# Neighbourhood bias as two Toeplitz strips per head and side, doubled tables, and Fourier operands loaded in three portions

## What is computed

```python
rows, kh = 16, 8
rstart = clip(r - kh // 2, 0, rows - kh)          # first of the 8 key rows of query row r
ridx = rstart[:, None] + arange(kh)[None, :]
cstart = clip(col - 8, 0, 64 - 16)                # 16 of the 64 key columns
cmask = (col >= cstart[:, None]) & (col < cstart[:, None] + 16)
dr_i = ridx - r[:, None] + 7
dc_i = clip(col[None, :] - col[:, None] + 15, 0, 30)
bias = rpb[:, dr_i[:, None, :, None], dc_i[None, :, None, :]]
s_loc = einsum(q, k[rows ridx]) * scale + bias    # masked with -1e30 outside cmask
p = softmax(concatenate([s_loc, s_ctx]))          # s_ctx: 512 cached keys, no bias
```

## Time and profile before

| | |
|---|---|
| median of 3 runs | 4331.23 us |
| the profiled execution's own time | 4325.63 us |
| its span | 4324.3 us |
| PE busy | 3974.8 us, 92% of the span |
| DVE, ACT, POOL busy | 2083.2, 902.7, 581.1 us |
| attention, first layer | about 433 us to 1018 us of the span |
| attention, second layer | about 2550 us to 3137 us |

### The profile page before, as it was taken

How to read it: one execution, slowest core, us unless ns; L and a number is a source line. 1 busy time by engine, 2 the same in 40 slices (tenths; PEclk the granted TensorE clock), 3 DMA queues, 4 the chain that set the end, 5 groups by cost and what they waited for, 6 DMA issues and landing times. The chain is left out here.

```text
span 4324.3 us, 48771 instructions
## 1 busy us (share of the span) xinstructions
PE 3974.8 (92%) x19072; PEld 3073.2 (71%) x19072; DVE 2083.2 (48%) x3396; ACT 902.7 (21%) x1700; POOL 581.1 (13%) x484
## 2 busy tenths in 40 slices
PE   5999899788989999999969989988979999999998
PEld 3788556555678888888848965555647888888885
DVE  4121555445265666665542235555444545544454
ACT  2111455343110000000021115543512000000002
POOL 1110111000021111111121110110101111111112
PEclk8999899899999999999979989999989999999999
DMA  6653423563212221111114433255540111110101
GB/s 235 201 161 118 105 52 83 138 170 104 83 52 61 69 69 59 60 57 64 49 30 144 149 102 95 47 130 134 135 153 19 39 40 40 39 40 30 38 31 49
DMA packets 306005, 375.69 MB, mean 87 GB/s; under 512 B 107570, under 2 KB 226228, under 8 KB 305648
## 3 DMA queue, kind: packets, MB, share of 16 engines
q1 hardware_dynamic: 285360, 367.59, 29.1%
q10 hardware_dynamic: 20416, 4.98, 0.5%
HBM read 304.01 MB, written 73.47 MB: 87 GB/s over the span
## 5 line engine op out<-in xcount | busy, mean ns | idle before, releaser
L1922 PE MATMUL bank<-h_hi,w_hi 128*128 128x512 f32 (+1 forms) x2448 | 902.5, 369 | 42.1 <-DVE h_lo L799 38.8
L1923 PE MATMUL bank<-h_lo,w_hi 128*128 128x512 f32 (+1 forms) x2448 | 871.8, 356 | 0.0
L1924 PE MATMUL bank<-h_hi,w_lo 128*128 128x512 f32 (+1 forms) x2448 | 871.2, 356 | 0.0
L2053 PE MATMUL bank<-prob,vv 128*128 128x512 f32 (+3 forms) x1504 | 714.3, 557 | 0.0
L1765 DVE SCALAR_TENSOR_TENSOR xT<-bank,mods,xT 128x512 f32<-128x512 f32 (+1 forms) x816 | 536.6, 660 | 349.2 <-PE bank L1924 331.4
L1922 PE MATMUL bank<-m_hi,w_hi 128*128 128x512 f32 (+1 forms) x1536 | 566.5, 369 | 51.8 <-DVE xT L1765 49.1
L1922 PEld LDWEIGHTS bank<-h_hi,w_hi 128*128 128x128 f32 x2448 | 465.6, 190 | 132.2 <-DVE h_lo L799 40.0
L1924 PE MATMUL bank<-m_hi,w_lo 128*128 128x512 f32 (+1 forms) x1536 | 545.3, 355 | 0.0
L1923 PE MATMUL bank<-m_lo,w_hi 128*128 128x512 f32 (+1 forms) x1536 | 544.6, 355 | 0.0
L1923 PEld LDWEIGHTS bank<-h_lo,w_hi 128*128 128x128 f32 x2448 | 465.4, 190 | 78.6 <-issue 14.5
L1924 PEld LDWEIGHTS bank<-h_hi,w_lo 128*128 128x128 f32 x2448 | 465.0, 190 | 65.9
(11 more groups left out here) (175 smaller groups left out, 4540.8 us busy)
## 6 DMA issues: line engine op xcount, KB each, us to landing
stage<-in_w_mlp SPq DMA_DIRECT2D x64, 1024.0 KB, 5.3
nx_w<-in_w_ada SPq DMA_DIRECT2D x16, 1536.0 KB, 7.1
stage<-in_w_in SPq DMA_DIRECT2D x18, 1024.0 KB, 6.1
ada_h<-in_w_ada SPq DMA_DIRECT2D x16, 1024.0 KB, 8.0
rope_t<-in_k_rope SPq DMA_DIRECT2D x28, 512.0 KB, 4.1
k<-s_kB SPq DMA_DIRECT2D x48, 224.0 KB
k<-s_kA SPq DMA_DIRECT2D x24, 448.0 KB, 10.6
k<-s_kD SPq DMA_DIRECT2D x24, 448.0 KB, 10.7
```

The lines of the kernel that those rows point to most:

```text
L1922: x = pe.matmul(out, a_hi, b_hi, start=first, stop=False)
L1923: pe.matmul(out, a_hi, b_lo, start=False, stop=False)
L1924: return x, pe.matmul(out, a_lo, b_hi, start=False, stop=last)
L2053: pe.matmul(ob[:, q0:q0 + n], vv[h % 2][:, key0 // P], prob[si % NP_RING][:, :n], start=(i == 0 and kind != "D"), stop=(i == len(steps) - ...
```

## The change

**Tables.** Each side of each head is now one table of 24 x 64 = 1536 columns. The first 14 x 64 columns serve query tiles at the edge (128 queries each; tiles 0, 1, 6 and 7), the last 10 x 64 columns the inner tiles (2 to 5). `BIAS_PARTS` lists four loads for each side: two of 64 x 896 and two of 64 x 512. Both sides are held twice, by the parity of the head.

**Work.** A tile at the edge now takes exactly its 512 keys (two pieces of 256 columns in place of two of 320). On the key side one step of each latent half of A shrinks from 512 to 256 queries. A key step that spans edge and inner tiles needs two additions on DVE, one for each strip.

**Order on SP.** All eight bias loads of the next head stand in turns 9 and 10 right behind `load_head`, ahead of the denominators. Ten of the Fourier loads move to the end of turn 8; the other four go in pairs (one of 1024 KB and one of 256 KB) to turns 12 and 13, behind `reciprocals`. The key loads that ended turns 8, 9 and 10 are gone.

```diff
-def na_pattern(t):
-    return {0: 0, 1: 1, 6: 3, 7: 4}.get(t, 2)
+FULL_ROWS, INNER_ROWS = 14, 10
+INNER0 = FULL_ROWS * GRID_W
+TABLE = (FULL_ROWS + INNER_ROWS) * GRID_W
+def at_edge(t):
+    return t in (0, 1, 6, 7)
+def table_col(t, row, key_side):
+    d = 2 * t - row + NA_KH - 1 if key_side else row - 2 * t + NA_KH - 1
+    return (d - 1) * GRID_W if at_edge(t) else INNER0 + (d - 3) * GRID_W
...
-            k0 = key_tile0(tt) * P
-            out += [(t, s, k0 + 320 * s, 320, (na_pattern(tt) * 640 + 320 * s)) for s in range(2)]
+            k0, n = (0 if tt < 2 else LAT // 2, 256) if at_edge(tt) else ((tt - 2) * P, 320)
+            out += [(t, s, k0 + n * s, n, table_col(tt, k0 // GRID_W, False) + n * s) for s in range(2)]
...
-            ts = [t for t in range(4) if key_tile0(4 * c + t) <= kt < key_tile0(4 * c + t) + 5]
+            ts = [t for t in range(4) if (kt // 4 == c if at_edge(4 * c + t) else abs(4 * c + t - kt) <= 2)]
...
+def bias_segments(c, kt, q0, n):
+    ts = range(4 * c + q0 // P, 4 * c + (q0 + n) // P)
+    runs = [[t for t in ts if at_edge(t) == e] for e in (True, False)]
+    return [((r[0] - ts[0]) * P, len(r) * P, table_col(r[0], 2 * kt, True)) for r in runs if r]
...
+BIAS_PARTS = [[(a, 0, 1 - a, FULL_ROWS) for a in range(2)] + [(a, INNER0 + (a + w) * GRID_W, 3 + w, NA_KH) for a in range(2)]
+              for w in range(2)]
...
+            def load_bias(h):
+                for w, tab, sm in ((0, na_q[h % 2], bq_in[h % 2]), (1, na_k[h % 2], bk_in[h % 2])):
+                    for half, c0, r, n in BIAS_PARTS[w]:
+                        sp.dma_start(tab[half * 64:half * 64 + 64, c0:c0 + n * GRID_W],
+                                     s_toe[l, h, w, :, r * GRID_W:(r + n) * GRID_W]).then_inc(sm, 16)
...
                 if v + 1 < NV:
                     load_head(v + 1)
+                if kind == "A" and 1 <= h < 3:
+                    sp.wait_ge(s1_max, l * PIECES + PIECE0[v * NCH])
+                    settle(sp)
+                    sp.wait_ge(s2_add, l * NADD + ADD0[v * NCH])
+                    load_bias(h + 1)
                 if v:
                     denominators_out(v - 1)
...
-                if kind == "A" and 1 <= h < 3:
-                    sp.wait_ge(s1_max, l * PIECES + PIECE0[(v - 1) * NCH + 2])
-                    load_bias(h + 1, 0)
                 if v:
                     reciprocals(v - 1)
-                if kind == "A" and h < 3:
-                    sp.wait_ge(s2_add, l * NADD + ADD0[v * NCH + 1])
-                    load_bias(h + 1, 1)
-                    sp.wait_ge(s2_add, l * NADD + ADD0[v * NCH + 2])
-                    load_bias(h + 1, 2)
+                if kind == "A" and h == 0:
+                    load_fourier()
...
-                    load_fourier()
+                if kind == "D" and h < 2:
+                    load_transform(h)
...
+                    for o, w, col in bias_segments(c, tab, q0, n):
+                        add = dve.tensor_tensor(sb[a % 2][:, o:o + w], bank[:, 2 + si % 3, o:o + w],
+                                                na_k[h % 2][:, col:col + w], ALU.add)
```

More of the change, by code:

```diff
@@ L53 @@
 NADA, NADA1 = 12, 4
[L56 to L62, removed]
 def constants():
@@ L531, in trunk @@
     off = W0
[L532 to L536, removed]
+    na_q, na_k = [], []
+    for s in range(2):
+        for lst, nm in ((na_q, "na_q"), (na_k, "na_k")):
+            a, off = at(f"{nm}{s}", [P, TABLE], F32, off)
+            lst.append(a)
+    off = W0 + 36864
     o_b, off = at("o_b", [P, 2, TOK], F32, off)
@@ L552, in trunk @@
     f_col, _ = at("f_col", [P, 2], F32, o + 32)
-    na_q1.append(put("na_q1b", [P, 2 * 640]))
+    cur["c"] += 2 * 640 * 4
     g_neg, _ = at("g_neg", [P, 2, 256], F32, cur["c"])
@@ L612, in trunk @@
     rest_in = [sem(f"rest_in{i}") for i in range(2)]
-    b_in = [sem(f"b_in{i}") for i in range(4)]
+    bq_in = [sem(f"bq_in{i}") for i in range(2)]
+    bk_in = [sem(f"bk_in{i}") for i in range(2)]
     b_init = sem("b_init")
@@ L966, in load_fourier, with load_transform @@
                 sp.dma_start(dft_col, I["k_dft_col"]).then_inc(f_in, 16)
[L967 to L969 removed]
+            def load_transform(x):
+                sp.dma_start(dft_t[:, x], I["k_dft_lat"][x].rearrange("(t p) n -> p t n", p=P)).then_inc(f_in, 16)
+                sp.dma_start(dft_x[:, x], I["k_dft_ctx"][x].rearrange("(t p) n -> p t n", p=P)).then_inc(f_in, 16)
             def load_head(v):
@@ L1185, in _ @@
             barrier(pool, l * PHASES + 1)
-            for tab in (na_q0, na_q1[0], na_q1[1], na_k[0], na_k[1]):
+            for tab in na_q + na_k:
                 pool.memset(tab, NEG).then_inc(b_init, 1)
@@ L1622, in _, with table_ready @@
             dve.wait_ge(lam_d, l * 5 + 5)
-            def table_ready(kind, h, which):
-                if kind == "A" and which == 0:
-                    n = 16 * len(BIAS_PARTS[0])
-                    dve.wait_ge(b_in[0 if h % 2 == 0 else 3], l * 2 * n + (h // 2 + 1) * n)
-                elif kind == "A":
-                    n = 16 * len(BIAS_PARTS[which])
-                    dve.wait_ge(b_in[which], l * 4 * n + (h + 1) * n)
+            def table_ready(sm, h):
+                n = 16 * len(BIAS_PARTS[0])
+                dve.wait_ge(sm[h % 2], l * 2 * n + (h // 2 + 1) * n)
             def piece(j, p):
@@ L1646, in piece @@
                 else:
-                    table_ready(kind, h, 0)
-                    table = q_table(h, tab, n) if kind == "A" else swa_q[:, tab:tab + n]
+                    if kind == "A":
+                        table_ready(bq_in, h)
+                    table = (na_q[h % 2] if kind == "A" else swa_q)[:, tab:tab + n]
                     if gi >= 2:
```

50 lines of the change are left out of this document (11 added, 39 removed).

## The result

| | before | after |
|---|---|---|
| median, timed side by side, 4 runs each | 4330.01 us (4328.18 to 4331.52) | 4279.46 us (4274.02 to 4281.96) |
| ratio | | 0.9879, 95% interval 0.9864 to 0.9894 |
| span of the profiled execution | 4324.3 us | 4280.6 us |

What follows compares the result with a forecast made beforehand. PE was taken as the bound, busy 92% of the span, with gaps from DVE waiting on late transfers. Terms 1 to 5 less term 6 gave 60.6 us, for a median of 4271 us, range 4250 to 4300.

Steps and rivals of the forecast that it cites:

- Term 1: Turns 9 and 10: `den_c` at T + 22.1 (T: previous head's scores done), not T + 28.8; 26.8 us.
- Term 2: Turn 11: head's loads wait only for six stores, `den_c` at T + 19.9, not T + 25.2; 10.6 us.
- Term 3: Turn 13: fewer Fourier loads ahead, `den_c` at T + 21.1, not T + 26.2; 10.2 us in both layers.
- The residual stalls of PE: PE's remaining stalls in turns 9 and 10, forecast at 3 to 5 us.
- term 5: PE in attention: narrower steps and pieces save 12 us of work, 7.5 us of it on the path.
- term 4: PE after stalls: shorter stalls give back half of 16 us lost to the low clock, 8 us.
- Term 6: DVE in A heads: 64 split additions cost 9.8 us, of which 2.5 us shows as loss.
- (a): Turns 9 and 10: bias loads cost `den_c` only 3 us and the clock does not fall; 4250 us; chance 0.15.
- (b): SP's queue: narrow load and slower bias bytes delay transfers, no clock back; 4303 us, half 4287; chance 0.16.
- (c): Slower: turns 9 and 10 get `den_c` at T + 33.4 or later, splits show; up to 4350 us; chance 0.04.
- (d): No change: DVE bounds the A heads and gives back the queue's gain; 4325 to 4335 us; chance 0.03.

Runs made afterwards that it cites:

- the repeat: The changed kernel run once more without any edit, beside the kernel before: 4274.84 us, ratio 0.9877.

## Why the prediction was right, and where its sizes were off

**Term 1, turns 9 and 10: right.** `den_c` was forecast at T + 22.1 and came at T + 21.5 and T + 21.6 (second layer: T + 22.2 and T + 20.6); `load_head` goes out at T, DVE waits once, 6.66 and 6.82 us. The mechanism is shown from both sides: without the later key loads the kernel before gains 33 us, and with the bias loads moved away the changed kernel gains another 29. The eight loads cost 5.4 us of landing (T + 16.1 in turn 8, T + 21.5 in turn 9), where 5.9 were taken, between 5.1 by the issue and 6.5 by the bytes. The wait for the bias loads is one for bytes in the queue: issuing the small store ahead of them changed nothing.

**Term 2, turn 11: right.** T + 19.8 (second layer T + 20.7) against T + 19.9.

**Term 3, turn 13: the landing was right, its price was not.** `den_c` came at T + 20.1 and T + 19.4, against T + 21.1, and k at T + 14.7, against "near T + 15". That is 6.2 and 5.7 us less for `den_c`, but the turn is only 3.2 and 3.0 us shorter. The term priced the landing of `den_c`, and before the change `den_c` held PE up by nothing there: PE's last wait was the one for k, which ended at T + 21.2. Now k comes early and PE goes on, and then stands still once more, until T + 20.9, for maxima that DVE writes after `den_c` (2.68 us; 3.12 in the second layer). Between the two it gets some 3.5 us of work done, and that is about the gain of the turn. Both layers together gave 6.2 us in place of 10.2 (8.0 in the repeat).

**The residual stalls of PE: too small.** In turns 9 and 10 they were put at 3 to 5 us and are 5.90 and 6.06. The prediction took PE to stall some 2 us less than DVE waits (it left 7 us for DVE); in the profile after, the difference is 6.66 - 5.90 = 0.8 us. With the widths of before the stalls are 4.83 and 4.97 us, so in the first layer 1.1 us of each is work ahead of the wait that PE is through with sooner (in the second, 5.59 and 5.05 stand against 6.54 and 4.97). That is the part of term 5 which the prediction itself had seen as lengthening the waits, and did not carry over to term 4.

**Term 4, the clock: the failed size.** Half of 16 us was taken as regained, because the stalls left would be at the edge of where the clock falls. All of them but one are beyond it: 0.50 from 788 to 792 us and 0.70 in the next 4, 0.51 from 828 to 832 behind the stall of turn 10, and in the second layer it falls behind the 3.19 us of turn 11, too. Only turn 11 of the first layer keeps 1.00. Added up from stretches of 1 us, PE worked 28.3 us at the low clock in turns 9 to 11 of both layers before, and 23.9 us after. At half the clock half of that is lost, so 2.2 us came back, in place of 8.

**Term 5, work: mostly right.** PE's busy time fell by 9.1 us (13.3 in the repeat), where 12 had been taken; putting the old widths back costs 5 to 6 us, where 7.5 was taken for the path.

**Term 6, the splits: right in being small.** 2.5 us were taken, and the runs can't tell that from nothing. On DVE itself the prediction had the work grow by 1.4 us; it fell by 5.7 (2083.2 to 2077.5). The 64 splits are worth 5.8 us of DVE's busy time, and not 9.8.

**The sum.** 60.6 us were forecast and 50.5 measured. In the profiles the whole gain lies in turns 8 to 13: 51.2 us, or 52.0 in the repeat. The 9.4 us that are short of 60.6 can be laid out by subtraction from these profiles. In turns 9, 10 and 11 DVE was free 38.1 us earlier, where terms 1 and 2 have 37.4. The clock gave back 2.2 us there, where term 4 has 8. Turn 13 gave 6.2, where term 3 has 10.2. What is left of turns 8 to 12 is 4.7 us, where terms 5 and 6 have 5.0; it is a remainder and not measured by itself. So the sum is short by the clock (5.8 us) and by turn 13 (4.0 us). Outside turns 8 to 13 the profiled execution is 7.5 us longer than the one of before, the repeat only 0.5 us, so the change doesn't make that.

**The rivals.** (a) fell with both its conditions: the loads cost 5.4 us and not 3, and the clock falls. Of (b), the two conditions on the queue fell: moving the narrow load changes nothing for `den_c`, and `den_c` comes no later than by 222 GB/s. Its third, no clock back, came close to true. (c) needed `den_c` at T + 33; it came at T + 21.5. (d) is refuted by the single addition, which shortens no stall, and by the 31 us that come from a later reciprocal with the same work on DVE.

## What to carry to other kernels

Count every wait of a stage from one common event, and read off when each transfer lands after it. What was queued on SP ahead of the small round trip here delayed it by its own bytes, whichever side of the store it stood on. A landing that comes earlier is worth only as much as the wait that ends last before and after: `den_c` of turn 13 came 6 us earlier and brought 3. Bulk loads belong behind the round trip and a turn ahead of their use. Taking a wait away shows the next one. Before the change the query table was through 6.6 us after `den_c` (T + 22.2 and T + 28.8 in turn 9), and a later reciprocal gave nothing; after the change it landed at T + 21.9 and T + 17.6 (turns 9 and 10, with the reciprocal later), about when `den_c` does or earlier, and the same edit gave 31 us. So look for all the waits at one place before choosing what to move.

## What the runs showed of the hardware

- A stall of PE of 2.34 us left the granted clock at 1.00 (turn 11); after one of 5.90 us it was at 0.50 for the first 4 us of work. Stalls hardly longer than 2.34 us did bring it down at the same place of other runs: 2.45 us with the denominators first, 2.64 us with one addition. The row is the 4 us after the first of these:

```profile
866.00:870.00 4.00, 4.00 (x12) 2.37 (x11) 2.13 (x7) 0.31 (x1) 0.00 (x0) 0.64 0.26 82
```

- In turn 13, after two stalls of 2.66 and 2.68 us with a few us of work between them, it fell to 0.51 as well (924 to 928 us), which had not been expected.
- The 5 KB of the denominators take 10.4 us from their issue until they have landed behind the head's and the bias loads (775.10 to 785.49), and their reading back 2.3 us (785.49 to 787.76). With the store earlier, the reading back alone took from 783.54 to 789.45, 2.43 us of it to issue.
- The 222 GB/s that the prediction took for all that the engines can move are what the head's loads of 64 partitions reach. The transform loads of turn 13 moved 323 GB/s at a busy share of 1.01 (928 to 932 us).
- The load of 127 partitions takes 4.45 us to issue where its neighbours take 0.3 to 0.5. `den_c` of turn 9 lands at T + 21.5 with it in turn 8 and without it there.
